# Order of the modulation's folds and start of the [hi|lo] products in a two-block kernel

## What is computed

```python
cs = jax.nn.silu(c)
mod = cs @ w_ada[l] + b_ada[l]
shift1, scale1, gate1, shift2, scale2, gate2 = [m[:, None, :] for m in jnp.split(mod, 6, axis=-1)]
h = _rmsnorm(x, norm1_g[l]) * (1.0 + scale1) + shift1
...
x = x + gate1 * (merged @ w_out[l])
h2 = _rmsnorm(x, norm2_g[l]) * (1.0 + scale2) + shift2
x = x + gate2 * _conv_ffn(h2, w_up[l], conv_w[l], conv_b[l], w_down[l])
```

## Time and profile before

| | us |
|---|---|
| median of 3 runs | 802.59 (802.23 to 802.83) |
| the profiled execution | 802.78 |
| its span, first to last instruction | 801.0 |
| TensorE busy | 791.0 (99%) |
| VectorE busy | 638.2 (80%) |
| ScalarE busy | 454.3 (57%) |
| granted TensorE clock, mean | 1.000 |

### The profile page before, as it was taken

The page is one execution under the profiler, slowest core; times in us unless marked ns, Lnnn a source line. Parts: engine busy times, 40 slices in busy tenths (PEclk is TensorE's granted clock), DMA queues, the critical chain, the costliest instruction groups (busy, mean ns, idle before and its releaser), DMA issues.

```text
span 801.0 us, 12246 instructions
## 1 busy us (share of the span) xinstructions
PE 791.0 (99%) x4888; PEld 704.6 (88%) x4888; DVE 638.2 (80%) x955; ACT 454.3 (57%) x649; POOL 32.1 (4%) x32
## 2 busy tenths in 40 slices
PE   7999999999999999999999999999999999999998
PEld 7899778889999888888888888889999988888887
DVE  4998999997888987776887898755777777777775
ACT  7848677637556345454876657775436644545451
POOL 2000000000000000000000000000000121111210
DMA  9996948964536866554354544444444555455411
GB/s 359 420 420 248 355 165 304 381 253 158 215 137 236 317 254 215 203 209 160 136 185 160 203 158 158 158 158 158 158 169 153 210 209 207 158 209 212 170 41 53
DMA packets 25480, 168.86 MB, mean 211 GB/s; under 512 B 2896, under 2 KB 3408, under 8 KB 5840
## 3 DMA queue, kind: packets, MB, share of 16 engines
q1 hardware_dynamic: 25280, 168.08, 56.7%
q10 hardware_dynamic: 144, 0.01, 0.0%
HBM read 167.03 MB, written 1.05 MB: 210 GB/s over the span
## 4 chain that ended last, share of the span: by engine, by line
PE 88%; DVE 7%; DMA 2%; ACT 2%; issue 1%; SPq 0%; ACTq 0%
PE ps L1761 46%; PE ps L1796 23%; PE ps L1803 12%; DVE wlo L1100 2%; PE ps L1857 2%; DVE raw L1066 1%; PE ps L2037 1%; DMA raw<-in_w_mem_kv 1%; ACT whi L516 1%; PE ps L2070 1%; PE ps L2008 1%; PE ps L2009 1%; DMA raw<-in_branches 1%; DVE wlo L1095 1%; DVE side_x L1066 0%
## 5 line engine op out<-in xcount | busy, mean ns | idle before, releaser
L1100 DVE TENSOR_TENSOR wlo<-raw,whi 128x2048 fp32r<-128x2048 f32 (+1 forms) x130 | 287.1, 2215 | 62.6 <-ACT whi L516 58.3
L516 ACT ACTIVATE whi<-raw 128x2048 fp32r<-128x2048 f32 (+2 forms) x144 | 251.0, 1756 | 82.2 <-PE ps L1796 42.6
L1796 PE MATMUL ps<-h_two,whi 128*128 128x512 f32 x512 | 123.8, 392 | 0.0
L1796 PEld LDWEIGHTS ps<-h_two,whi 128*128 128x128 f32 x512 | 94.1, 188 | 18.3
L1761 PE MATMUL ps<-h_two,whi 128*128 128x256 f32 x544 | 99.3, 285 | 1.8 <-DVE wlo L1095 1.6
L1761 PEld LDWEIGHTS ps<-h_two,whi 128*128 128x128 f32 x544 | 84.7, 192 | 2.8 <-DVE wlo L1095 1.8
L1761 PE MATMUL ps<-h_two,wlo 128*128 128x256 f32 x272 | 76.9, 283 | 0.0
L1761 PE MATMUL ps<-whi,fhi 128*128 128x512 f32 (+1 forms) x178 | 69.1, 388 | 0.0
L1761 PE MATMUL ps<-whi,flo 128*128 128x512 f32 (+1 forms) x178 | 68.9, 387 | 0.0
L1761 PE MATMUL ps<-wlo,fhi 128*128 128x512 f32 (+1 forms) x178 | 68.8, 387 | 0.0
L1796 PE MATMUL ps<-g_two,whi 128*128 128x512 f32 x288 | 68.4, 390 | 0.0
(11 more groups left out here) (278 smaller groups left out, 1424.1 us busy)
## 6 DMA issues: line engine op xcount, KB each, us to landing
raw<-in_w_up SPq DMA_DIRECT2D x44, 1024.0 KB, 4.8
raw<-in_w_in SPq DMA_DIRECT2D x43, 1024.0 KB, 4.8
raw<-in_w_down SPq DMA_DIRECT2D x22, 1024.0 KB, 4.8
raw<-in_w_ada SPq DMA_DIRECT2D x14, 1024.0 KB, 5.2
raw<-in_branches SPq DMA_DIRECT2D x10, 1024.0 KB, 4.8
raw<-in_w_out SPq DMA_DIRECT2D x4, 1024.0 KB, 6.9
raw<-in_w_o SPq DMA_DIRECT2D x4, 1024.0 KB, 4.7
raw<-in_w_mem_kv SPq DMA_DIRECT2D x3, 1024.0 KB, 11.2
```

The costliest lines, as they stand in the source:

```text
L516: return nc.scalar.activation(dst, src, func, **kw)
L1100: V.tensor_tensor(wlo[:, w % SPLIT, c:UNIT], raw[:, slot, c:UNIT], f32(whi[:, w % SPLIT, c:UNIT]), ALU.subtract).then_inc(raw_done, 1)
L1796: ins = mm(ps[:, b, :], wt(whi, w, kt, P * i, P, 256), two[:, :, kt, :], start=start and kt == 0, stop=stop and kt == KT - 1, skip_group_c ...
```

## The change

Three things are changed. The plan: pieces 16 to 19 (scale2) are folded where 12 to 15 (shift2) were, 12 to 14 behind BR1+0 to BR1+2, nothing behind BR1+3, and 15 behind FFN1+0; pieces 20 to 23 behind FFN1+15, +18, +21 and +24 instead of +9, +12, +15 and +18. The shift's copy and its high and low extra columns move from ahead of the projection into its second and third step, on VectorE and on ScalarE. In the first feed-forward paired units begin at column pair 3 instead of 4, and the banks of its paired a and g units are exchanged.

```diff
--- before.py
+++ after.py
@@ -64,9 +64,9 @@
 
     plan.extend(START_PLAN)
     w = MEMKV + 4 + FIRST
-    after = {WIN1 + at: (a,) for a, at in enumerate((9, 12, 13, 14, 15, 16, 17, 18, 19, 20), 10)}
-    after[WIN1 + 10] = (9,)
-    after.update({FFN1 + at: (a,) for a, at in enumerate((9, 12, 15, 18), 20)})
+    behind = {9: 10, 10: 9, 12: 11, 13: 16, 14: 17, 15: 18, 16: 19, 17: 12, 18: 13, 19: 14, FFN1 - WIN1: 15}
+    after = {WIN1 + at: (a,) for at, a in behind.items()}
+    after.update({FFN1 + at: (a,) for a, at in enumerate((15, 18, 21, 24), 20)})
     while w < NW:
         weights(1)
         plan.extend(("ada", a) for a in after.get(w - 1, ()))
@@ -140,8 +140,8 @@
 WIDE = S + 2
 WIDE_BANKS = {("a", 0): (0, 6), ("g", 0): (1, 5), ("a", 1): (7, 4), ("g", 1): (2, 3)}
 BCAST = 256
-FIRST_PAIRED = (4, 2)
-PAIRED_A, PAIRED_G = ((0, 1), (0, 1)), ((2, 3), (2, 3))
+FIRST_PAIRED = (3, 2)
+PAIRED_A, PAIRED_G = ((2, 3), (0, 1)), ((0, 1), (2, 3))
 
 
 def ring_slot(entry):
@@ -832,7 +832,7 @@
                     round_unit(o0 + u + AHEAD)
                     if u == 2:
                         copy(eps_root, eps, ACT.Sqrt)
-                    if k == 0 and u == 0:
+                    if k == 0 and u == 2:
                         act.wait_ge(sem("shift_ready"), 1)
                         copy(wide_hi[:, :, S:WIDE], mod[:, 24:32].unsqueeze(2).to_broadcast([P, KT, 2]))\
                             .then_inc(sem("wide_hi_ready"), 1)
@@ -1444,11 +1444,6 @@
                 return gs2[:, c:c + 1]
 
             gains(gs2, 4, "norm2_g")
-            dve.wait_ge(raw_done, ada_folded(3))
-            V.tensor_copy(shift_out, mod[:, 24:32]).then_inc(sem("shift_ready"), 1)
-            dve.wait_ge(sem("wide_hi_ready"), 1)
-            V.tensor_tensor(wide_lo[:, :, S:WIDE], mod[:, 24:32].unsqueeze(2).to_broadcast([P, KT, 2]),
-                            f32(wide_hi[:, :, S:WIDE]), ALU.subtract).then_inc(sem("wide_lo_ready"), 1)
             dve.wait_ge(sem("x_landed"), 16)
             dve.wait_ge(raw_done, ada_folded(2))
             for u in range(4):
@@ -1478,6 +1473,13 @@
                 if u in (1, 2):
                     sum_squares("two", SQUARES["two"], mg, u - 1)
                     split_low(w + AHEAD)
+                if u == 1:
+                    dve.wait_ge(raw_done, ada_folded(3))
+                    V.tensor_copy(shift_out, mod[:, 24:32]).then_inc(sem("shift_ready"), 1)
+                if u == 2:
+                    dve.wait_ge(sem("wide_hi_ready"), 1)
+                    V.tensor_tensor(wide_lo[:, :, S:WIDE], mod[:, 24:32].unsqueeze(2).to_broadcast([P, KT, 2]),
+                                    f32(wide_hi[:, :, S:WIDE]), ALU.subtract).then_inc(sem("wide_lo_ready"), 1)
             invert("two")
             split_low(FFN1 + 2)
             split_low(FFN1 + 3)
```

## The result

The changed kernel takes 806.10 us (median of 7 executions, 804.11 to 806.23) against 802.59 (802.23 to 802.93, 7 executions). The ratio is 1.0035, 95% interval 1.0025 to 1.0044; on 802.59 that is 805.4. It is slower, by 0.35%. The executions fall in two groups, and the granted TensorE clock parts them: 804.11 and 804.28 us at a mean clock of 1.000, and 805.58, 806.10, 806.11, 806.16 and 806.23 at 0.998. The profiled one (806.11 us, span 804.3) is of the second group.

A forecast was written before the change was run, and what follows sets the result against it. The prediction took TensorE to bound the kernel, busy 791.0 of 801.0 us, so only its products' cost and new waits count. A new wait of 2.1 less 0.43 from pairing gave +1.67 us, 804.3; range 803.2 to 805.8.

The forecast's parts named there:

- Part 1: Branches: one fold leaves, others are reordered; the 2.41 us saved on VectorE are not on TensorE's path, worth 0.
- Part 2: Projection: piece 15's fold delays the shift's low half, so TensorE's first wide unit waits 2.1 us (bounds 1.7 to 2.4).
- Part 3: SP's load queue: FFN1+1 to FFN1+4 asked for one split later, still in time; cost 0, up to a few tenths.
- Part 4 and 5: First feed-forward: later folds of pieces 20 to 23 cost 0; pairing pair 3 takes its step from 16.98 to 16.55, gain 0.43 us.
- The extra wait of g3: Unit g3 needs pair 2's gate product; without piece 20's fold ahead, 1.1 us to spare, else up to 1.3 us lost.
- The sum, 804.3: Whole kernel: +2.1 - 0.43 = +1.67 us, giving 804.3 on the median.
- a second wait: Rival: unit g3 waits for the gate product or a load lands late; 1.1 to 2.4 us more, 805.4 to 806.7, chance 0.11.
- another rival: The prediction's range counts "the half-way case of the second rival"; it does not spell out which rival that is.
- the clock falls after the new wait: Rival: behind the first wide unit's wait, one 5.76 us unit takes twice as long, giving 810; chance 0.03.

The follow-up runs named there:

- pair_late: Kernel before with paired pair 3 and pieces 20 to 23 folded later; order of pieces 12 to 19 and shift as before: 802.16 us, ratio 0.9999.
- pair_only: Kernel before with only pairing from column pair 3 and exchanged banks; pieces 20 to 23 in their old places: 803.60 us, ratio 1.0013.
- filled: Changed kernel with 20 identity transposes on TensorE ahead of its wait for the shift's low half: 804.09 us.
- half_early: Changed kernel with only the shift's low half written earlier, ahead of the sum and split of FFN1+1; fold stays: 804.85 us, median of 8.
- spot_free: Changed kernel with the shift early again, pieces 12 and 13 behind BR1+1 and BR1+2, 14 and 15 behind BR1+3: 803.10 us, ratio 1.001.
- fold15_only: Kernel before with only the new order of pieces 12 to 19 (15 behind FFN1+0) and the late shift: ratio 1.0037.
- dose3: Changed kernel with piece 15 behind BR1+3, shift still late, three extra 1,024-column sums on VectorE ahead of its low half: 807.53 us.

## Why the prediction was right, and where it was not

- *Part 1, the branches, 0:* right. pair_late keeps the old order and comes out at the same time.
- *Part 2, the wait:* right, step by step. Forecast and measured: tiles 0 and 1 at 185.83 and 185.89; the split of FFN1+0 at 191.66 and 191.72; tiles 4 and 5 at 196.5 and 196.54; the low half at 201.9 and 201.92; the first wide product at 202.1 and 202.19. The wait was forecast as 2.1; the list says 2.05.
- *Part 3, the loads, 0:* right; the changed kernel has no new wait for a load.
- *Part 4 and 5:* right. 16.55 forecast, 16.56 measured. The extra wait of g3 that the late folds avoid was put at up to 1.3 us; pair_only shows 1.37.
- *The sum, 804.3:* right for executions whose clock stays up (804.11, 804.28), too low by 1.8 for the others (median 806.11), which are five of seven. The ratio gives 805.4, within the range 803.2 to 805.8; the median of all seven, 806.10, lies 0.3 above the range. That 805.4 falls within it is in part luck: the upper part of the range was there for a second wait and for half of another rival, neither of which came, and not for the clock.
- *The step that failed* is the rival "the clock falls after the new wait". Its mechanism was right and both its sizes were wrong. I gave it a chance of 0.03; it came in 5 of 7. And I priced it at a whole unit at half speed, 5.8 us; it cost 1.55. The chance rested on one row: behind a wait of 1.62 us the clock had stayed at 1.00. The runs show why that row could not carry it. At 1.2 and 1.37 us the clock stayed up in 22 of 22 executions too, at 2.05 it fell in 8 of 12 and at 3.71 in 5 of 5. One case on the harmless side says nothing of a wait that is longer. The same trace had a case on the other side that the prediction does not use: behind the 4.24 us without work at the start, products ran at half pace until 11.4 us, which PEclk doesn't show. The Trainium skill, page "TensorE: Matmul & The Clock Gate", section "HAM oscillation — how this bites in real kernels", has the rule that TensorE should have no idle gap above a certain length, as its clock is lowered behind one. The trace of the changed kernel agrees that a gap does this, with 0.42 us in place of 0.28 for a product behind it, and filled shows that the gap is the cause. It does not agree on the length: the limit that the Trainium skill gives lies above 2.05 us, and the clock fell behind that wait in 8 of 12 executions. The measurement decides.

What stays open: why the clock falls in one execution and stays in the next, with the same wait (two of seven here), what made two shorter waits with little work between them enough in half_early, if it was these, and what brought the clock down in the one execution of spot_free. No run tells these apart.

## What to carry to other kernels

Where TensorE runs without a gap, other engines' work is free only up to the next instruction that TensorE waits for; lay out that engine's chain up to there, and count what stands ahead of a small instruction, not the instruction itself. Price a new wait of TensorE with what follows it: here 2.05 us cost 3.6 in most executions, as the clock fell behind it. Where such a wait could not be avoided, work without use in it kept the clock up and won back the second part. And look at the pitch of the products beside the mean clock, which here says nothing of the slow start.

## What was not expected of the hardware

- One new wait of 2.05 us brought the granted clock from 1.00 to 0.5 (2.4 to 1.2 GHz) in 8 of 12 executions. In the profile of the changed kernel it fell 1.15 us after the work had begun again and cost 1.55 us; in that of fold15_only it fell after 0.56 us, and behind the 3.71 us of dose3 it was down when work began.
- Filling the wait with 20 transposes of a constant kept it at 1.000 in 11 of 11, at 804.09 us against 806.10 for the changed kernel.
- ScalarE's wait for one load of the branches' weights was 1.56 to 3.63 us in the 14 profiled executions, and TensorE waited up to 1.3 us for what hung on it. This is probably one source of the spread between executions; no run shows how much of it.
